# Block 1's mixers: projections in the recurrence's order, six half steps of the inverse among them, unread products taken out

## The chip, the cores and the metric

The kernel runs on one core of one Trainium2 chip. The metric is device microseconds (us) of one execution. Five engines work side by side, each through its own queue and in order: PE (TensorE, matrix products; PEld is its weight load), DVE (VectorE), ACT (ScalarE), POOL (GpSimd) and SP (SyncE, which issues the loads). They wait for each other through semaphores. `ps` is the accumulation memory that products land in, eight banks of 128 x 512 floats; `SB`, `SA`, `HT`, `XT`, `SM` and others are named parts of the on-chip memory.

## What is computed

256 tokens of width 1024 go through two blocks. The first block is a stack of two layers. Each layer projects its input onto the columns of three mixers, runs the mixers, joins their outputs with `w_out`, and ends with a gated feed-forward part:

```python
def first_block(x, ...):
    for l in range(DEPTH):                                   # 2
        h = x @ w_cols
        h_gla, h_rwkv, h_nsa, h_vres = _split(h, ...)
        o_gla = _gla_mixer(gq, gk, gv, gg, galr, ...)        # linear attention, 4 heads, chunks of 64
        o_rwkv = _rwkv7_mixer(rr, rk, rv, ...)               # recurrence, 4 heads, state 64 x 64
        o_nsa = _nsa_mixer(h_nsa, pos, ...)                  # block attention, 8 heads, 2 key heads
        mix = jnp.concatenate([o_gla, o_rwkv, o_nsa], axis=-1) @ w_out[l]
        x = _layer_norm(DEEPNORM_ALPHA * x + mix, ln1_w[l], ln1_b[l])
        ffn = (jax.nn.silu(x @ ffn_w_gate[l]) * (x @ ffn_w_up[l])) @ ffn_w_down[l]
        x = _layer_norm(DEEPNORM_ALPHA * x + ffn, ln2_w[l], ln2_b[l])
    return x
```

The recurrence runs over tokens, `state = state * w_t + sa * b_t + v_t * k_t`. The kernel solves it by chunks of 128 tokens, for which a triangular matrix for each chunk and head is inverted. Block attention is three attentions over the same queries (15 compressed key blocks, selected blocks, a window), each with a gate.

The second block modulates its input by sums over a condition vector (`mod = c @ w_ada + b_ada`), has a mixer of its own, and then a feed-forward part of 32 experts with 4 chosen for each token. All of it is float32.

## The kernel before

**Loads.** SyncE streams all weights through `ring`, four slots of 2 MB, in a fixed order (`ORDER`): for each layer of the first block 7 slots of projections, 2 of the compression, 2 of `w_out`, 11 of gate and up, 6 of down. Twelve slots of the modulation (`ada`) of the second block are put behind slots that `ADA_BEHIND` names; for each, VectorE runs four multiply-and-sum operations (L1704, `modulation_dve`). The condition row that they need is loaded by `condition_sp`, and the rows made of the sums go out through `modulation_rows_sp`, behind a turn on TensorE (`modulation_turn_pe`).

**Projections.** `project_pe` (from L384) makes 15 groups, each a bank of `ps`: weights on the left (L401) for the transposed columns, and for groups 11 to 14 tokens on the left (L418). ScalarE evacuates each (`proj_evac`), and group g needs the evacuation of group g - 4. The columns come in the order linear attention's queries and keys, then the recurrence's R, K, V, ranks, then attention's keys and queries. `rwkv_norm_pe`, `rope_pe` (L1001, the product that rotates keys and queries) and `rwkv_bonus_pe` (L737) stand between the last groups.

**Mixers.** `mixers_pe` (L2571), `mixers_act` and `mixers_dve` write the order of the mixers out by hand. First come eight score products of linear attention (`gla_scores_pe`, L504; VectorE makes a key for each ahead of it, `gla_key_dve`, and masks them all behind the last, `gla_mask_dve`, up to L583), with four pairs of the recurrence's matrices (`rwkv_pairs_pe`, L759) and the compression's hidden layer (`cmp_hidden_pe`, L1048) among them. Then a loop of `STEPS` = 18 steps runs three things side by side:
- the inverse of the recurrence's triangles, for two chunks in turn, in 14 half levels. A half step is a product (`inverse_product_pe`, L858), copied by ScalarE (L892), and an update (`inverse_update_pe`, L877 and L880), added in by VectorE (`inverse_update_dve`, L843). Half levels 0 and 1 are made by masks, 2 to 13 in steps 0 to 11 (`h = s + FIRST_HALF`), and then come six steps of the solve with it: `chunk_removed`, `chunk_solve`, `chunk_out` for each chunk;
- attention in 12 units (`NU`), each four heads of one chunk of queries: 4 with 256 keys, 4 with 128, 4 with the 15 compressed ones. A unit's scores are made in step u + 2 (L1149); VectorE masks them (L1221) or copies them (L1220), ScalarE takes the exponential, VectorE scales them by sum and gate in the next step (L1241 to L1250), TensorE turns them (L1166), ScalarE copies them, and a step later TensorE makes the output (L1177);
- the rest of linear attention in steps 0 to 2.

`clock_pe` (L357 to L360) makes products of constants into a bank whose contents nobody reads; several calls stand in these functions, and they are called fillers below.

Behind the loop the recurrence's output gets its head norm on VectorE (`rwkv_norm_dve`, L457 to L468 and to L972) while TensorE starts `w_out` (L1272): `mix_early_pe` with the six parts k of `EARLY`, which need `gla_out` and `nsa_out`, and `mix_late_pe` with k 2 and 3, which need `rw_out`. Then come layer norm and the gate, up and down products (L1403, L1488), and the next layer, which is the same.

## Time and profile before

| what | us |
|---|---|
| median of 3 runs | 2024.41 |
| the three runs | 2035.28, 2024.41, 2023.99 |
| the profiled execution | 2022.85 |
| its span in the trace | 2021.0 |
| its mean granted TensorE clock | 0.993 |

The profile shows one execution. The span is cut into 40 slices of 50.5 us, and each digit is the busy share of an engine in tenths (DMA is the mean share of the 16 DMA engines, PEclk the clock that TensorE was granted, in tenths of its full 2.4 GHz):

```profile
PE   8999999999999999999999999999999999999997
DVE  2387588774587586764731111111111111111112
PEclk9999999999999999999999999999999999999999
DMA  8440057656630065437299999999999999999996
```

Slices 1 to 10 are layer 0 of the first block, slices 10 to 19 layer 1, then comes the second block's mixer, and from slice 22 on the experts. The chain that ended last, followed back from the last instruction, gives each line's share of the span:

```profile
PE 80%; DMA 15%; DVE 3%; issue 1%; ACT 0%; SPq 0%; DVEq 0%
```

In the rows below, `L858 PE` is line 858 of the kernel on TensorE, `ps<-SB` the program's names for what is written and read, `128*128 128x128` the weights' and the moving operand's shape, and `x8` the number of instructions drawn together. Each float32 product of the program leaves two records.

### The profile page before, as it was taken

What the parts mean: (1) busy time and instruction counts of PE and PEld (TensorE: products, weight loads), DVE (VectorE), ACT (ScalarE), POOL (GpSimd) and SP (SyncE); (2) the same over time, 40 slices, a digit from 0 to 9 for tenths busy, and PEclk for the clock granted to TensorE, in tenths of its full rate; (3) what the DMA queues carried; (4) which work ended last, traced back from release to release, by engine and by line L of the source; (5) the groups of instructions that cost most, each with busy time, mean ns of one, the idle gap of its engine ahead of it and who ended that gap; (6) DMA issues with size and microseconds to landing.
All of it is one profiled execution on the core that took longest, in us unless ns stands there. A gap on an engine that the chain in (4) does not pass through costs nothing.

```text
span 2021.0 us, 24513 instructions
## 1 busy us (share of the span) xinstructions
PE 1965.7 (97%) x9835; PEld 1113.9 (55%) x9835; DVE 854.5 (42%) x1538; ACT 313.5 (16%) x725; POOL 45.1 (2%) x62
## 2 busy tenths in 40 slices
PE   8999999999999999999999999999999999999997
PEld 7867588848878588748653333333333333333332
DVE  2387588774587586764731111111111111111112
ACT  1335211101435121102410000000000000000001
POOL 0021000000021000000000000000000000000000
PEclk9999999999999999999999999999999999999999
DMA  8440057656630065437299999999999999999996
GB/s 362 182 163 3 32 219 302 229 208 248 266 153 1 22 240 198 167 134 280 105 363 400 429 427 429 428 428 428 428 429 428 429 428 429 428 428 429 428 428 291
DMA packets 44275, 598.75 MB, mean 296 GB/s; under 512 B 5056, under 2 KB 5360, under 8 KB 8464
## 3 DMA queue, kind: packets, MB, share of 16 engines
q1 hardware_dynamic: 44208, 597.82, 71.9%
q8 instruction: 46, 0.75, 0.1%
q14 instruction: 21, 0.17, 0.0%
HBM read 596.73 MB, written 1.07 MB: 296 GB/s over the span
## 4 chain that ended last, share of the span: by engine, by line
PE 80%; DMA 15%; DVE 3%; issue 1%; ACT 0%; SPq 0%; DVEq 0%
PE ps L2348 18%; DMA ring<-in_stream 15%; PE ps L1403 13%; PE ps L2396 8%; PE ps L401 6%; PE ps L1488 5%; PE ps L2322 3%; PE ps L1272 3%; PE ps L360 2%; PE ps L2337 2%; PE ps L418 2%; PE ps L2433 2%; PE ps L1819 1%; PE ps L1985 1%; PE ps L1149 1%; PE ps L1166 1%
## 5 line engine op out<-in xcount | busy, mean ns | idle before, releaser
L2348 PE MATMUL ps<-ring,HT 128*64 128x512 f32 x2176 | 478.9, 594 | 16.9 <-DMA ring<-in_stream 16.4
L2348 PEld LDWEIGHTS ps<-ring,HT 128*64 128x64 f32 x2176 | 152.9, 137 | 336.4 <-issue 290.9
L2396 PE MATMUL ps<-SB,HT 128*64 128x512 f32 x1088 | 252.4, 618 | 0.9 <-ACT HT L2459 0.9
L2504 DVE TENSOR_SCALAR HT<-ps 128x512 f32<-128x512 f32 x34 | 23.5, 691 | 446.1 <-PE ps L2348 446.1
L2396 PEld LDWEIGHTS ps<-SB,HT 128*64 128x64 f32 x1088 | 77.7, 142 | 172.9 <-issue 172.9
L1403 PE MATMUL ps<-ring,SB 128*128 128x256 f32 x704 | 156.0, 379 | 0.3 <-DVE SB L330 0.3
L2453 ACT ACTIVATE HT<-HT 128x512 f32<-128x512 f32 x34 | 21.4, 630 | 843.6 <-DVE HT L2504 843.6
L1403 PEld LDWEIGHTS ps<-ring,SB 128*128 128x128 f32 x704 | 133.6, 190 | 18.8 <-issue 0.7
L2516 DVE TENSOR_TENSOR HT<-ps,TOK 128x512 f32<-128x512 f32 x34 | 23.5, 691 | 284.6 <-PE ps L2396 284.6
L401 PE MATMUL ps<-SB,ring 128*128 128x256 f32 x576 | 126.5, 382 | 3.4 <-DMA ring<-in_stream 3.4
L401 PEld LDWEIGHTS ps<-SB,ring 128*128 128x128 f32 x576 | 110.3, 192 | 19.3 <-DMA ring<-in_stream 2.5
L1403 PE MATMUL ps<-SB 128*128 128x256 f32 x352 | 80.0, 379 | 0.4 <-ACT SB L345 0.4
L1704 DVE SCALAR_TENSOR_TENSOR ring<-ring,SB 128x1024 f32<-128x1024 f32 x48 | 55.8, 1219 | 43.9 <-DMA ring<-in_stream 43.9
L1403 PEld LDWEIGHTS ps<-SB 128*128 128x128 f32 x352 | 66.7, 190 | 9.8 <-issue 0.8
L2337 PE MATMUL ps<-SA,HT 32*64 32x512 f32 x272 | 69.7, 608 | 0.0
L2433 PE MATMUL ps<-HT 64*128 64x512 f32 x272 | 67.6, 615 | 0.9 <-DVE HT L2516 0.9
L2322 PEld LDWEIGHTS ps<-HT,SA 128*128 128x128 f32 x512 | 59.6, 192 | 13.0 <-DVE HT L2442 13.0
L2322 PE MATMUL ps<-HT,SA 128*128 128x128 f32 x512 | 64.0, 278 | 0.0
L1488 PE MATMUL ps<-ring,HT 128*128 128x512 f32 x132 | 60.4, 592 | 0.0
L1272 PE MATMUL ps<-ring,SB 128*128 128x512 f32 x128 | 56.4, 596 | 1.6 <-DVE SB L2709 1.6
L360 PE MATMUL ps<-CST 128*128 128x256 f32 (+2 forms) x190 | 52.0, 393 | 0.0
L2442 DVE TENSOR_TENSOR HT<-ps,COND 128x512 f32<-128x512 f32 x32 | 22.1, 691 | 68.5 <-PE ps L2322 68.5
(489 smaller groups left out, 2249.0 us busy)
## 6 DMA issues: line engine op xcount, KB each, us to landing
ring<-in_stream SPq DMA_DIRECT2D x210, 2048.0 KB, 17.5
SB<-in_stream SPq DMA_DIRECT2D x68, 2048.0 KB, 25.6
SB<-in_ln SPq DMA_DIRECT2D x8, 512.0 KB, 6.9
CST<-in_const SPq DMA_DIRECT2D x1, 1362.0 KB, 5.3
PAR<-in_layer SPq DMA_DIRECT2D x2, 558.5 KB, 11.6
X<-in_x SPq DMA_DIRECT2D x1, 1024.0 KB, 4.9
SB<-in_cond_row SPq DMA_DIRECT2D x2, 512.0 KB, 5.3
HN<-in_head_norm SPq DMA_DIRECT2D x2, 512.0 KB, 12.5
```

The costliest lines, as they stand in the source:

```text
L360: pe.matmul(ps[:, b, at:at + width], ident, cst("pairs")[:, 0:width], start=True, stop=True)
L401: m = pe.matmul(ps[:, proj_bank(g), j * T:(j + 1) * T], w[:, k, (2 * (g % 2) + j) * P:(2 * (g % 2) + j + 1) * P], XT[:, k, :], start=k == ...
L418: m = pe.matmul(ps[:, proj_bank(g0 + t), 0:n], XT[:, k, t * P:(t + 1) * P], w[:, k, a:a + n], start=k == 0, stop=k == KT - 1)
L1272: m = pe.matmul(ps[:, 2 * t + c, :], OT[:, k, t * P:(t + 1) * P], w[:, k, :], start=start and k == ks[0], stop=stop and k == ks[-1], skip_ ...
L1403: ins = pe.matmul(gate_products(f, (m,)), left[:, k, :], right[:, k, :], start=k == 0, stop=k == 3)
L1488: ins = pe.matmul(ps[:, DOWN_BANK[m], :], left, right, start=s + q == 0, stop=s == 5)
L1704: ins = nc.vector.scalar_tensor_tensor(out=w[:, b, :], in0=w[:, b, :], scalar=1.0, in1=CB, op0=ALU.mult, op1=ALU.mult, accum_out=ACC[:, 4 ...
L2322: m = pe.matmul(ps[:, 2, (k % 4) * P:(k % 4 + 1) * P], HF[:, t, k * P:(k + 1) * P], EP0[:, t, :, :].rearrange("p a s -> p (a s)"), start=t ...
L2337: pe.matmul(ps[HD * half:HD * (half + 1), a, :], EOW[0:NE, q, :], BGU[0:NE, half, a, :], start=True, stop=False, skip_group_check=True)
L2348: m = pe.matmul(ps[HD * half:HD * (half + 1), a, :], XE[:, 2 * b + k, q * SLOTS_E:(q + 1) * SLOTS_E], w[:, k, a, half, :], start=False, st ...
L2396: m = pe.matmul(ps[HD * c:HD * (c + 1), 3, :], EHT[:, k, HD * b:HD * (b + 1)], w[:, k, c, :], start=b + k == 0, stop=b + k == 4, skip_grou ...
L2433: m = pe.matmul(ps[:, 4 + 2 * t + c, :], EPT[rows, t * P:(t + 1) * P], EY[rows, :], start=False, stop=True, skip_group_check=True)
```

## The change

- **Columns and groups.** The weights' columns are put in the order R, K, V, ranks, one compression value, then linear attention's queries and keys, then attention's. VectorE's first step on the recurrence (`mix_dve`) waits for five evacuations instead of seven.
- **Projections interleaved.** New functions `projections_pe`, `projections_act` and `projections_dve` write the order of the projections out by hand. Between groups 7 to 14 stand the recurrence's norm, bonus and pairs, the four rotations (all through bank 4 now), the first half levels, and half steps 2 and 3.
- **Mixers.** Half steps 4 to 7 stand between the eight score products. The loop starts at half step 8 (`LOOP_HALF`) and has 16 steps; the solve's six steps stand in steps 6 to 11. The recurrence's norm is in VectorE's step 12 (`BACK - 2`), its way back in TensorE's step 14, and the first `w_out` part in step 15.
- **`w_out`.** The early parts are k 0 to 3 now, for three of four quarters, and wait for `rw_out` and `gla_out`; the late ones are k 4 to 7 and the whole last quarter, and wait for `nsa_out`. Other banks of `ps` take them.
- **Fillers.** All calls of `clock_pe` go, but for one in `chunk_removed_pe`.
- **Modulation.** One block instead of two stands in layer 0's projections, behind the third slot; the others move to layer 0's gate stage, layer 1's projections and layer 1's gate stage, and none stands in layer 0's down projection. The turn of the sums and SyncE's rows move from layer 1's gate stage to its down projection.
- GpSimd's masks of the half levels lose their waits for attention; the compression's blocks move to another place in memory.

The core of the diff:

```diff
-ADA_BEHIND = {("in", 0, 1): (0, 1), ("gu", 0, 2): (2,), ("gu", 0, 4): (3,), ("gu", 0, 6): (4,), ("gu", 0, 8): (5,),
-              ("dn", 0, 0): (6,), ("dn", 0, 1): (7,), ("in", 1, 1): (8, 9), ("in", 1, 3): (10, 11)}
+ADA_BEHIND = {("in", 0, 2): (0,), ("gu", 0, 2): (1,), ("gu", 0, 4): (2,), ("gu", 0, 5): (3,), ("gu", 0, 7): (4,), ("gu", 0, 8): (5,),
+              ("in", 1, 1): (6, 7), ("gu", 1, 2): (8,), ("gu", 1, 4): (9,), ("gu", 1, 6): (10,), ("gu", 1, 8): (11,)}
...
+                if name == "in" and l == 0 and s == 2:
+                    condition_sp(sp)
                 if name == "gu" and s == 1:
                     norm_params(sp, 2 * l)
-                    if l == 0:
-                        for done in ("gla_out", "rw_out", "nsa_out"):
-                            sp.wait_ge(S(done), 1)
-                        condition_sp(sp)
-                if name == "gu" and s == 4 and l == DEPTH - 1:
+                    for done in ("gla_out", "rw_out", "nsa_out"):
+                        sp.wait_ge(S(done), l + 1)
+                    condition_sp(sp)
+                if name == "dn" and s == 4 and l == DEPTH - 1:
                     modulation_rows_sp(sp)
...
-            v.wait_ge(S("proj_evac"), 15 * l + 7)
+            v.wait_ge(S("proj_evac"), 15 * l + 5)
...
-                pe.wait_ge(S("proj_evac"), 15 * l + 13)
+                pe.wait_ge(S("proj_evac"), 15 * (l + 1))
...
-            if s == 2:
-                pe.wait_ge(S("cmp_x"), l + 1)
...
-        EARLY = (0, 1, 4, 5, 6, 7)
-
-        def mix_early_pe(pe, l, t, c, ks=EARLY):
+        def mix_early_pe(pe, l, t, c):
+            pe.wait_ge(S("rw_out"), l + 1)
+            pe.wait_ge(S("gla_out"), l + 1)
+            mix_part_pe(pe, l, t, c, range(4), True, False)
+
+        def mix_late_pe(pe, l):
             pe.wait_ge(S("nsa_out"), l + 1)
-            mix_part_pe(pe, l, t, c, ks, ks[0] == 0, False)
-
-        def mix_late_pe(pe, l):
-            pe.wait_ge(S("rw_out"), l + 1)
-            for t in range(NT):
-                for c in range(2):
-                    if (t, c) == (1, 0):
-                        mix_early_pe(pe, l, 1, 1, EARLY[3:])
-                    m = mix_part_pe(pe, l, t, c, (2, 3), False, True)
-                m.then_inc(S("mix_ready"), 1)
+            mix_part_pe(pe, l, 0, 0, range(4, 8), False, True)
+            mix_part_pe(pe, l, 0, 1, range(4, 8), False, True).then_inc(S("mix_ready"), 1)
+            mix_part_pe(pe, l, 1, 1, range(4, 8), False, True)
+            mix_part_pe(pe, l, 1, 0, range(8), True, True).then_inc(S("mix_ready"), 1)
...
-        FIRST_HALF, HALF_LEVELS, ATT_LAG = 2, 14, 2
-        STEPS = HALF_LEVELS - FIRST_HALF + 6
+        FIRST_HALF, LOOP_HALF, HALF_LEVELS, ATT_LAG = 2, 8, 14, 2
+        STEPS = NU + 2 + ATT_LAG
         CMP_TURN, CMP_OUT, GLA_NORM, GLA_BACK = 0, 1, 1, 2
+        BACK = NU + ATT_LAG
...
+        def inverse_step_pe(pe, l, h):
+            inverse_product_pe(pe, l, h + 1)
+            inverse_update_pe(pe, l, h)
+
+        def projections_pe(pe, l):
+
+            for g in range(0 if l == 0 else 2, 7):
+                project_group_pe(pe, l, g)
+            gla_gate_pe(pe, l)
+            rwkv_ranks_pe(pe, l)
+            project_group_pe(pe, l, 7)
+            rwkv_norm_pe(pe, l)
+            project_group_pe(pe, l, 8)
+            rope_pe(pe, l, 0)
+            project_group_pe(pe, l, 9)
+            rwkv_bonus_pe(pe, l)
+            rwkv_pairs_pe(pe, l, 0)
+            project_group_pe(pe, l, 10)
+            rwkv_pairs_pe(pe, l, 2)
+            rope_pe(pe, l, 1)
+            project_group_pe(pe, l, 11)
+            rwkv_pairs_pe(pe, l, 4)
+            project_group_pe(pe, l, 12)
+            rope_pe(pe, l, 2)
+            rwkv_pairs_pe(pe, l, 6)
+            inverse_first_pe(pe, l, 0)
+            project_group_pe(pe, l, 13, range(4))
+            inverse_first_pe(pe, l, 1)
+            project_group_pe(pe, l, 13, range(4, KT))
+            rope_pe(pe, l, 3)
+            inverse_product_pe(pe, l, FIRST_HALF)
+            project_group_pe(pe, l, 14, range(2))
+            inverse_step_pe(pe, l, 2)
+            project_group_pe(pe, l, 14, range(2, 5))
+            inverse_step_pe(pe, l, 3)
+            project_group_pe(pe, l, 14, range(5, KT))
+            rwkv_current_pe(pe, l)
+
         def mixers_pe(pe, l):
-            pe.wait_ge(S("rope"), ROPE_PIECES * l + 2)
-            for u in range(8):
-                gla_scores_pe(pe, l, u)
-                if u % 2 == 0:
-                    rwkv_pairs_pe(pe, l, u)
-                if u == 0:
-                    rwkv_current_pe(pe, l)
-                if u + 2 < ROPE_PIECES:
-                    rope_pe(pe, l, u + 2)
-                    clock_pe(pe, 0, 384, P, 4)
-                else:
-                    pe.wait_ge(S("rope"), ROPE_PIECES * l + 3)
-                    clock_pe(pe, 7, 0, 256, 1)
+            gla_scores_pe(pe, l, 0)
+            inverse_step_pe(pe, l, 4)
+            gla_scores_pe(pe, l, 1)
+            gla_scores_pe(pe, l, 2)
+            inverse_step_pe(pe, l, 5)
+            gla_scores_pe(pe, l, 3)
+            gla_scores_pe(pe, l, 4)
             cmp_hidden_pe(pe, l, 0)
-            inverse_first_pe(pe, l)
+            inverse_step_pe(pe, l, 6)
+            gla_scores_pe(pe, l, 5)
+            gla_scores_pe(pe, l, 6)
             cmp_hidden_pe(pe, l, 4)
-            inverse_product_pe(pe, l, FIRST_HALF)
+            inverse_step_pe(pe, l, 7)
+            gla_scores_pe(pe, l, 7)
             for s in range(STEPS):
                 u, at = s - ATT_LAG, NU * l + s - ATT_LAG
-                h = s + FIRST_HALF
+                h = s + LOOP_HALF
...
+                elif j < 2:
...
+                if s == BACK + 1:
+                    mix_early_pe(pe, l, 0, 0)
...
+                if s == BACK:
+                    back_pe(pe, 2 * l + 1, R_XC, 5)
+            mix_early_pe(pe, l, 0, 1)
+            mix_early_pe(pe, l, 1, 1)
...
+        def projections_dve(v, l, I, L):
+            mix_dve(v, l, I, L)
+            rwkv_square_dve(v, l, I, L)
+            gla_bias_dve(v, l, I)
+            rwkv_prepare_dve(v, l, I, L)
+            rwkv_mask_dve(v, l, 0)
+            rwkv_mask_dve(v, l, 1)
+            rope_dve(v, l, 0, I, L)
+            rwkv_mask_dve(v, l, 2)
+            rwkv_mask_dve(v, l, 3)
+            inverse_first_dve(v, l, 0)
+            rope_dve(v, l, 1, I, L)
+            rwkv_mask_dve(v, l, 4)
+            rwkv_mask_dve(v, l, 5)
+            gla_decay_dve(v, l, I, L)
+            rwkv_mask_dve(v, l, 6)
+            rwkv_mask_dve(v, l, 7)
+            inverse_first_dve(v, l, 1)
+            inverse_turned_dve(v, l, 0)
+            inverse_turned_dve(v, l, 1)
+            rope_dve(v, l, 2, I, L)
+            gla_query_dve(v, l, I)
+            inverse_update_dve(v, l, 2)
+            rope_dve(v, l, 3, I, L)
+            inverse_update_dve(v, l, 3)
             gla_key_dve(v, l, 0)
             gla_key_dve(v, l, 1)
-            rope_dve(v, l, 0, I, L)
-            rope_dve(v, l, 1, I, L)
-            for u in range(8):
-                rwkv_mask_dve(v, l, u)
-                if u == 0:
-                    rwkv_init_dve(v, l, I, L)
-                if u + 2 < NQC:
-                    gla_key_dve(v, l, u + 2)
-                if u + 2 < ROPE_PIECES:
-                    rope_dve(v, l, u + 2, I, L)
-            v.wait_ge(S("rw_mm"), 8 * (l + 1))
-            inverse_first_dve(v, l)
-            inverse_turned_dve(v, l)
+            rwkv_init_dve(v, l, I, L)
+
+        def mixers_dve(v, l, I, L):
+            for h in range(4, 7):
+                inverse_update_dve(v, l, h)
+                gla_key_dve(v, l, 2 * h - 6)
+                gla_key_dve(v, l, 2 * h - 5)
+            inverse_update_dve(v, l, 7)
...
+                if s == BACK - 2:
+                    rwkv_norm_dve(v, l, I, L)
...
-            rwkv_norm_dve(v, l, I, L)
             v.wait_ge(S("back_ps"), 2 * l + 2)
             nc.vector.tensor_copy(OT[:, 2:4, :].rearrange("p c t -> p (c t)"), ps[:, 5, :]).then_inc(S("rw_out"), 1)
+            attention_merge_dve(v, NU * (l + 1), I)
```

What this does to the order of the instructions is shown at three places. Line numbers of the kernel after differ; `x4` counts the program's instructions here, two records each in the trace.

**TensorE, the last projections (L418, group 13) and the first scores of linear attention (L504).** L1001 is a rotation, L737 turns the recurrence's operands, L745 sums its bonus, L759 a pair of the recurrence, L360 a filler. Before:

```order
L418 MATMUL ps<-ring,SB 128x512 x8
L737 MATMUL ps<-CST,SB 128x128 x4
L504 MATMUL ps<-HT,SA 128x32 x4
L759 MATMUL ps<-SB 128x256 x4
L745 MATMUL ps<-PAR,SB 128x4 x4
L1001 MATMUL ps<-HT,CST 128x256 x2
L360 MATMUL ps<-CST 128x128 x4
```

After, at the same group (L399 is the projection, L790 a first half level's turn, L970 a rotation, L833 a half step's product, L850 and L853 its update):

```order
L399 MATMUL ps<-ring,SB 128x512 x4
L790 MATMUL ps<-CST,SB 128x128 x4
L399 MATMUL ps<-ring,SB 128x512 x4
L970 MATMUL ps<-HT,CST 128x256
L833 MATMUL ps<-SB 128x128 x4
L399 MATMUL ps<-ring,SB 128x512 x2
L833 MATMUL ps<-SB 128x128 x4
L850 MATMUL ps<-SB 128x128 x4
L853 MATMUL ps<-SB 128x128 x4
L399 MATMUL ps<-ring,SB 128x512 x3
```

The filler and the scores are gone from here, and half steps stand between the quarters of the last two groups.

**TensorE, a step of the loop amid the attention units with 128 keys.** L1149 is the scores, L360 a filler, L858 a half step's product, L877 and L880 its update, L1177 the output and L1166 the turn of earlier units. Before:

```order
L1149 MATMUL ps<-HT 128x128 x4
L360 MATMUL ps<-CST 128x256
L858 MATMUL ps<-SB 128x128 x4
L877 MATMUL ps<-SB 128x128 x4
L880 MATMUL ps<-SB 128x128 x4
L1177 MATMUL ps<-SA,NV 64x256 x4
L1166 MATMUL ps<-CST,SA 128x128 x4
```

After (L1118 scores, L888 the solve's product in place of a half step, L1146 output, L1135 turn):

```order
L1118 MATMUL ps<-HT 128x128 x4
L888 MATMUL ps<-SB 128x64 x4
L1146 MATMUL ps<-SA,NV 64x256 x4
L1135 MATMUL ps<-CST,SA 128x128 x4
L1118 MATMUL ps<-HT 128x128 x4
```

The step keeps the scores, output and turn, and has four products of the solve instead of a filler and a half step of twelve.

**VectorE, the recurrence's head norm (L457 to L468 and on) and the last attention units.** L1250 is the scaling of a unit, L1256 the merge of attention's outputs, L952 a copy of the solve. Before:

```order
L1250 TENSOR_TENSOR SA<-SA,SM 128x4x15
L958 TENSOR_SCALAR SB<-ps,SM 64x64 x4
L946 COPY SB<-ps 128x256
L1256 COPY SB<-ps 128x4x128 x2
L952 COPY SB<-ps 128x256
L457 TENSOR_REDUCE SM<-ps 128x8
L458 TENSOR_SCALAR SM<-SM 128x8
L459 TENSOR_TENSOR SB<-ps,SM 128x512
```

After (L945 is the end of the norm, which starts 12 rows ahead at L438; L1184 masks a unit's scores, L1192 to L1219 scale it):

```order
L945 TENSOR_TENSOR SB<-SB 128x512
L1184 TENSOR_TENSOR SA<-ps,CST 128x4x15
L1192 TENSOR_REDUCE SM<-SA 128x4
L1201 TENSOR_SCALAR SM<-SM 128x4
L1210 RECIPROCAL SM<-SM 128x4
L1214 TENSOR_TENSOR SM<-SM,SB 128x4
L1217 TENSOR_SCALAR SM<-SM,CST 128x4
L1219 TENSOR_TENSOR SA<-SA,SM 128x4x15
```

Before, the norm stands behind the last scaling and the merge. Now it stands ahead of the last two units' scaling.

## Rows read from the trace of the kernel before

**Rows 1.** The page's busy times of the engines, share of span, instructions.
```profile
PE 1965.7 (97%) x9835; PEld 1113.9 (55%) x9835; DVE 854.5 (42%) x1538; ACT 313.5 (16%) x725; POOL 45.1 (2%) x62
```

**Rows 2.** Table by stage: window, us; engines' busy us (count); PEclk, DMA share, GB/s.
```profile
569.40:594.30 24.90, 24.26 (x251) 18.03 (x250) 18.23 (x33) 6.18 (x15) 11.12 (x20) 1.00 0.29 96
594.30:674.80 80.50, 78.78 (x650) 64.82 (x650) 59.62 (x132) 41.21 (x131) 9.72 (x8) 1.00 0.12 50
1100.00:1990.00 890.00, 865.37 (x4142) 319.26 (x4140) 154.80 (x335) 49.90 (x93) 0.00 (x0) 0.99 1.01 428
```

**Rows 3.** Time line of TensorE, layer 1: start, us, line, [idle before <-releaser].
```profile
569.44 0.63 PE L504 MATMUL ps<-HT,SA 64*128 64x32 f32 x8
...
594.35 1.16 PE L858 MATMUL ps<-SB 128*128 128x128 f32 x8 [0.69 <-ACT SB L892]
...
674.83 5.42 PE L1272 MATMUL ps<-ring,SB 128*128 128x512 f32 x12
...
707.75 7.14 PE L1403 MATMUL ps<-ring,SB 128*128 128x256 f32 x32 [0.16 <-DVE SB L330]
```

**Rows 4.** The same time line: a half step between its ends.
```profile
640.16 1.05 PE L858 MATMUL ps<-SB 128*128 128x128 f32 x8
...
642.93 1.08 PE L1177 MATMUL ps<-SA,NV 128*64 128x256 f32 x8
```

**Rows 5.** Time lines of VectorE and TensorE: mask, units with 256 keys, update.
```profile
592.71 0.68 DVE L583 TENSOR_TENSOR SA<-ps,CST 128x512 f32<-128x512 f32 x1
...
621.52 0.69 DVE L1220 COPY SA<-ps 128x512 f32<-128x512 f32 x1 [1.08 <-PE ps L1149]
...
624.58 1.22 DVE L1250 TENSOR_TENSOR SA<-SA,SM 128x1024 f32<-128x1024 f32 x1
...
625.73 1.28 DVE L843 TENSOR_TENSOR SB<-SB,ps 128x512 f32<-128x512 f32 x2
...
628.07 0.69 DVE L1220 COPY SA<-ps 128x512 f32<-128x512 f32 x1 [1.06 <-PE ps L1149]
...
625.86 1.09 PE L1166 MATMUL ps<-CST,SA 128*128 128x128 f32 x8 [0.50 <-DVE SA L1250]
```

**Rows 6.** The same time lines: units with 128 keys.
```profile
633.42 0.72 PE L1149 MATMUL ps<-HT 64*128 64x128 f32 x8
...
654.68 0.62 PE L1149 MATMUL ps<-SB,HT 64*128 64x15 f32 x8
...
645.30 0.69 DVE L1221 TENSOR_TENSOR SA<-ps,CST 128x512 f32<-128x512 f32 x1 [0.97 <-PE ps L1149]
...
647.23 0.69 DVE L1250 TENSOR_TENSOR SA<-SA,SM 128x512 f32<-128x512 f32 x1
```

**Rows 7.** The same time lines: unit 10's scores, the recurrence's norm.
```profile
660.66 0.62 PE L1149 MATMUL ps<-SB,HT 64*128 64x15 f32 x8
...
682.89 0.69 DVE L457 TENSOR_REDUCE SM<-ps 128x8 f32<-128x512 f32 x1 [7.53 <-PE ps L938]
...
690.31 0.69 DVE L972 TENSOR_TENSOR SB<-SB 128x512 f32<-128x512 f32 x1
```

**Rows 8.** Table by stretch of line 360 alone: PE and PEld busy us.
```profile
569.40:594.30 24.90, 6.30 (x28) 3.88 (x28) 1.00 0.29 96
594.30:674.80 80.50, 13.33 (x48) 8.07 (x48) 1.00 0.12 50
```

**Rows 9.** Time line of TensorE: the start, and two items of the experts.
```profile
10.90 29.36 PE L401 MATMUL ps<-SB,ring 128*128 128x256 f32 x128 [1.27 <-DMA ring<-in_stream]
...
42.36 41.71 PE L401 MATMUL ps<-SB,ring 128*128 128x256 f32 x192 [2.10 <-DMA ring<-in_stream]
...
1167.68 8.74 PE L2396 MATMUL ps<-SB,HT 128*64 128x512 f32 x32
...
1224.70 7.09 PE L2396 MATMUL ps<-SB,HT 128*64 128x512 f32 x32
```

**Rows 10.** TensorE's waits, 400 to 470 us: us in total, times, longest.
```profile
PE ps L1488 <- DVE HT L1465: 2.2, 3, 1.5
```

More of the change, by code:

```diff
@@ new lines, in project_group_pe @@
+        def project_group_pe(pe, l, g, ks=range(KT)):
+            s = min(g // 2, 6) if g < 11 else 5 + (g > 12)
+            need_slot(pe, AT["in", l, s])
+            w = slot(AT["in", l, s]).rearrange("p (k n) -> p k n", k=KT)
+            if g >= 4:
+                pe.wait_ge(S("proj_evac"), 15 * l + g - 3)
+            for j in range(2 if g < 10 else 1):
+                for k in ks:
+                    if g < 11:
+                        at = (2 * (g % 2) + j) * P
+                        left, right, to = w[:, k, at:at + P], XT[:, k, :], slice(j * T, (j + 1) * T)
+                    else:
+                        t, cols = (g - 11) % 2, slice(P, P + 280) if g < 13 else slice(0, 512)
+                        left, right, to = XT[:, k, t * P:(t + 1) * P], w[:, k, cols], slice(0, 280 if g < 13 else 512)
+                    m = pe.matmul(ps[:, proj_bank(g), to], left, right, start=k == 0, stop=k == KT - 1)
+            if ks[-1] == KT - 1:
+                m.then_inc(S("proj_ready"), 1)
@@ L647, in rwkv_ranks_pe @@
                               start=False, stop=True)
+            if l:
+                pe.wait_ge(S("gla_zb"), l + 1)
+                for c in range(2):
+                    m = pe.matmul(ps[:, 4, c * T:(c + 1) * T], par("misc")[M_VR:M_VR + 32, c * P:(c + 1) * P],
+                                  HT[M_VR:M_VR + 32, T_MISC, :], start=True, stop=True)
             m.then_inc(S("rw_z"), 1)
@@ new lines, in inverse_first_dve, with turned_triangle, inverse_first_pe @@
+            v.wait_ge(S("rw_mk"), 12 * l + s + 1)
+            nc.vector.tensor_tensor(TT[:, us, :], MK[:, us, :], idb, ALU.add).then_inc(S("rw_tm"), 1)
+        def turned_triangle(s):
+            return ps[:, (7, 6)[s], :]
+        def inverse_first_pe(pe, l, s):
+            pe.wait_ge(S("rw_bk"), l + 1)
+            pe.wait_ge(S("rw_mk"), 12 * l + s + 1)
+            for i in range(4):
+                m = pe.transpose(turned_triangle(s)[:, i * P:(i + 1) * P], MK[:, 4 * s + i, :], ident)
+            m.then_inc(S("rw_z_ps"), 1)
```

265 lines of the change are left out of this document (93 added, 172 removed).

## Prediction

> **What bounds the kernel now.** The page's busy times first [rows 1]: TensorE is "busy" for 97% of the span, so that number can't say where time is lost, since products whose result nobody reads are in it. The table by stage [rows 2] can. From 1100 to 1990 us the DMA share is 1.01 at 428 GB/s: the experts' weights set the pace, and the change doesn't touch that stage. Its loads start when the blocks ahead have finished, so what a layer gains or loses ahead of it is carried to the end one for one. In the two stretches of the mixers the DMA share is 0.29 and 0.12: something else sets their pace.
>
> The time line of layer 1 shows the stage's marks [rows 3]. (Layer 0 has the same pattern 452.4 us earlier, so each term counts twice.) Up to 569.4 TensorE runs projections back to back without a wait. From 569.44 to 594.35 it runs eight score products of linear attention, four pairs of the recurrence and fillers; at 594.35 the loop of half steps and attention begins; at 674.83 w_out; at 707.75 the feed-forward part.
>
> In that loop TensorE looks full and isn't what paces it. For a unit with 256 keys VectorE starts at 621.52 and starts the next at 628.07 [rows 5]: 6.55 us. The circle is: VectorE copies, masks, reduces and scales until 625.80 (L1250, 624.58 + 1.22); TensorE turns the unit before (625.86, with a wait of 0.50 for just this), makes the next scores, and VectorE goes on. The update of the inverse (L843, 1.28 us) and the half step's products (2.77 us, [rows 4]) lie inside this circle for nothing.
>
> **The change, part by part, for layer 1.**
>
> 1. Six half steps of the inverse go from the loop to places between projections and scores. One costs TensorE 642.93 - 640.16 = 2.77 us [rows 4]. Where they stood, they were covered by the circle above; among the projections TensorE has no hole, so there they cost all of it: 6 x 2.77 = **+16.6**. The projections themselves, the pairs, the rotations and the compression keep their number and size, and their order costs nothing: I followed who waits for whom. The recurrence's first groups are ready after five evacuations, VectorE's preparation runs under groups 7 to 9, and GpSimd's masks under 13 and 14.
>
> 2. The 28 filler records between 569.4 and 594.3 go: 6.30 us of records [rows 8], less the modelled overlap of eight groups, **-5.7**.
>
> 3. New waits. Behind half steps 4, 5 and 6 VectorE runs the update (1.28, [rows 5]) and only then the next key (at most one operation of L1220's size, 0.69, and half of it for the early keys), while TensorE has 0.55 or 1.0 us of scores to cover it. Three waits of about 1.2, 1.5 and 1.0: **+3.7**. Nothing else on TensorE can pass them, since it runs in order.
>
> 4. The mask of the scores (three operations, the last L583 ending 593.39 [rows 5]) was over 1.0 us before the loop's first product at 594.35. Now the last score stands directly ahead of the loop and VectorE has update 7 to do first, so the mask ends 1.9 us behind it; VectorE then goes into the compression's gelu, which is what the loop's second step waits for. I take **+2.8**. A filler that stood ahead of a transpose in the third step goes: -0.4.
>
> Attention starts 16.6 - 5.7 + 3.7 + 2.8 - 0.4 = 17.0 us later.
>
> 5. The four units with 256 keys: the circle has no half step in it, so it stays 6.55: **0**.
>
> 6. The four units with 128 keys take 654.68 - 633.42 = 21.3 us [rows 6] with half steps and fillers; there TensorE is full. Without them the circle decides: VectorE from 645.30 to 647.92 (L1250, 647.23 + 0.69, [rows 6]) = 2.6, turn 0.6, scores 0.65, handovers 0.15: 4.0 us. The first has still a wide unit to scale (5.0), and the one with the solve's output products (2.5 us) 4.3. So 5.0 + 4.0 + 4.4 + 4.0 = 17.4: **-3.9**.
>
> 7. The recurrence's output comes in step 11, amid the four narrow units: 2.2 us of products in a step of 2.9, **+0.9**. Its norm (L457 to L972, 682.89 to 691.00, 8.1 us [rows 7]) ran under w_out's first products. Now VectorE has it in step 12, and the last two attention units are queued behind it; TensorE has nothing but their transposes to do. From the end of unit 10's scores (660.66 + 0.62) to w_out was 13.5 us [rows 3, 7]. It becomes 1.5 (unit 9's scaling) + 8.1 + about 5 us for two units one after the other, the way back and a copy = 14.6: **+1.1**. So the two steps that the loop loses are given back here.
>
> 8. From the first w_out product to the feed-forward part was 32.9 us [rows 3]. The 64 records are 27.5 of it; the solve's last outputs, a filler, a wait for the norm's copy and the way back are now ahead of it: 29.3, **-3.6**.
>
> Sum per layer: 17.0 - 3.9 + 0.9 + 1.1 - 3.6 = **+11.5**.
>
> 9. The clock. Without fillers TensorE stands idle for about 8 us under the norm, and for 1.5 to 3 us in many steps. What the trace has nearest: at the start, behind 5.9 us of nothing, 128 records take 29.4 us where 192 later ones take 41.7 [rows 9], that is 1.6 us lost; and in the expert stage the same 32 records take 8.74 us in one item and 7.09 in another [rows 9], where the granted clock went to 0.5, the 1.2 GHz level, behind short waits: 1.65 us. The bounds are 0 (the granted clock is 1.00 through the layers now) and all TensorE work between 650 and 700 at half rate, 12 us, less what the waits swallow, say 10. I take one loss of 1.6 behind the norm, 1.3 for the two transposes and products right behind it that are on the path, and one dip of 1.65 in the steps: **+4.5**, nearer the low end, as one dip is what the rows show at a time.
> The Trainium skill, "TensorE: Matmul & The Clock Gate", Part 1, says that the half rate is the default and that activity releases it, and it advises against holes between bursts of matmuls. This speaks against taking the fillers out. With it the sum has the 4.5; without it 0 there, and the total would be 9 us lower.
>
> 10. Start of layer 0: the second block of the modulation goes, and the first comes behind the third slot. The wait of 2.10 us at 42.36 [rows 9] goes: **-2.1**, once. In the down projection of layer 0 TensorE waits 2.2 us for sums that VectorE makes late because of modulation blocks [rows 10]; those go: **-2.2**, once. In the gate stage of layer 0 five blocks stand instead of four, two pairs of them in neighbouring steps. VectorE then needs 13.1 us in each where TensorE needs 12.5, and is 4 us ahead: nothing. In layer 1 the four blocks stand as layer 0's did. SyncE's wait for the modulation rows moves to the down projection, ahead of one load that isn't due by then: nothing.
>
> Total: 2 x (11.5 + 4.5) - 2.1 - 2.2 = **+27.7**. Against the profiled execution (time 2022.85, span 2021.0, both in the table of times; 1.6 below the median of the runs) this is 2050.5; I say **2050 us**.
>
> **Rivals.**
> - *The same, and the clock holds.* For it: 1.00 throughout the layers now, and steps that stay more than half full. 2 x 11.5 - 4.3 = +18.7: 2041.
> - *The clock stays low through much of attention.* For it: every step there has a hole now. About 10 a layer in place of 4.5: 2061 to 2066.
> - *TensorE's queue paces the loop after all*, and the waits of 0.5 us are the accident. Then the fillers (13.3 us of records in the loop, [rows 8], and 6.3 ahead of it) come off the path, the half steps cost nothing net, and a layer loses 12 to 18 us: 2022.85 - 30 - 4.3 = about 1985. Against it: the 0.50 wait recurs at the same place in each wide step, and VectorE's circle adds up to the step. It decides from the point where attention starts less than 8 us later.
> - *The norm doesn't hold attention up* (part 7 is off by 8 us) and the waits of part 3 are half: 2 x (11.5 - 8 - 1.9) - 4.3 = -1: about 2022 to 2028.
>
> **Chances.** Forecast 0.50; clock holds 0.26; clock low 0.10; norm free 0.08; TensorE paces 0.06. About 1% (20 us) is what a measurement of this kernel tells from no change; measured from the median 2024.4 the bound lies at 2044.7, inside the spread of the forecast's own case (2041 to 2058), of which I give a tenth to "within". Slower: 0.45 + 0.10 + 0.04 of the clock-holds case = 0.59. Faster: 0.06, and 0.01 of the norm case: 0.07. Same: 0.34. The range takes in the clock-holds case and most of the clock-low one, with 5 us a layer of error in parts 3, 4 and 7 below: 2031 to 2064.
>
> **What would show it.** Part 1: the linear-attention scores begin some 14 us later after the start of the projections than 569.44 - 480. Part 3: TensorE waits of 1 to 1.5 us ahead of the scores, ended by VectorE's key. Part 5: units with 256 keys 6.5 us apart. Part 6: units with 128 keys 4 us apart. Part 7: a TensorE wait of about 8 us ended by L1219, the scaling. Part 9: a granted clock under 1.00 there. Wrong would be: the first attention scores of layer 1 less than 10 us later than now after the projections' start, or an expert stage that takes the shift up.

## The result, and the profile after

The changed kernel takes 2064.53 us (median of 4 executions, 2062.54 to 2068.92). The kernel before took 2024.2 in the same comparison. The ratio is 1.0195, 95% interval 1.0167 to 1.0222: it is slower by 40 us, about 2%. The prediction said 2050 with a range up to 2064. The side was right, the median lies half a microsecond above the range's upper end, and the change cost one and a half times what was forecast.

The page of the profiled execution (2068.92 us, span 2067.1, mean granted clock 0.975 where it was 0.993) shows the busy times that answer to [rows 1], and the row of the granted clock over the 40 slices of the span:

```profile
PE 1962.3 (95%) x9687; PEld 1106.0 (54%) x9687; DVE 852.0 (41%) x1539; ACT 315.2 (15%) x725; POOL 46.1 (2%) x62
PEclk9998899999999799999999999999999999999999
```

Before, all 40 digits were 9. Now slices 4 and 5 (layer 0's mixers) and slice 14 (layer 1's) are lower. In the experts' stage all digits are 9 as before.

The table by stage of TensorE in layer 1 of the kernel after, which answers to [rows 2]. Columns: window, its length, TensorE's busy time (records), granted clock, DMA share, GB/s. The windows run from the start of the projections to the first score, the loop, the first, fifth, ninth and eleventh attention unit's scores, `w_out`, and the feed-forward part:

```profile
486.70:604.90 118.20, 118.20 (x625) 1.00 0.44 175
604.90:634.00 29.10, 25.19 (x258) 0.88 0.34 117
634.00:647.60 13.60, 10.93 (x100) 0.98 0.50 214
647.60:677.50 29.90, 19.96 (x143) 0.84 0.00 1
677.50:697.40 19.90, 19.00 (x141) 0.82 0.01 2
697.40:704.50 7.10, 6.94 (x63) 1.00 0.02 4
704.50:721.50 17.00, 7.01 (x45) 0.62 0.19 61
721.50:753.10 31.60, 31.44 (x77) 0.93 0.06 18
```

In the kernel before every one of these stretches had 1.00. Five of the eight are now well below it. TensorE's waits over the whole execution (engine, what, line <- who, line: us in total, times, longest) name who it stands for:

```profile
PE ps L1135 <- DVE SA L1219: 31.8, 15, 7.5
PE ps L485 <- DVE SA L560: 7.0, 6, 1.4
```

L1135 is the turn of an attention unit, L1219 VectorE's scaling of it (in [rows 5] L1166 and L1250), L485 a score product of linear attention and L560 its key. In the kernel before, the same view has no wait for a key, and for the scaling only six short ones:

```profile
PE ps L1166 <- DVE SA L1250: 2.8, 6, 0.5
```

### The profile page after: what moved, and what is told of

The parts are those of the page before. It is cut to its first block, busy times and chain, and to the rows that moved or that the text cites. A ratio compares the mean times of both kernels' runs of the same rounds, so it can differ in the third digit from the quotient of the medians.

```text
span 2067.1 us, 24237 instructions
## 1 busy us (share of the span) xinstructions
PE 1962.3 (95%) x9687; PEld 1106.0 (54%) x9687; DVE 852.0 (41%) x1539; ACT 315.2 (15%) x725; POOL 46.1 (2%) x62
## 4 chain that ended last, share of the span: by engine, by line
PE 79%; DMA 14%; DVE 5%; issue 1%; ACT 0%; SPq 0%; DVEq 0%
PE ps L2315 17%; DMA ring<-in_stream 14%; PE ps L1372 12%; PE ps L399 9%; PE ps L2363 8%; PE ps L1456 6%; PE ps L2289 3%; PE ps L1244 3%; PE ps L2304 2%; PE ps L2400 2%; PE ps L1786 1%; PE ps L1952 1%; PE ps L1135 1%; PE ps L1118 1%; PE ps L833 1%
## 5 line engine op out<-in xcount | busy, mean ns | idle before, releaser
L2471 DVE TENSOR_SCALAR HT<-ps 128x512 f32<-128x512 f32 x34 | 23.5, 692 | 449.9 <-PE ps L2315 449.9
L2483 DVE TENSOR_TENSOR HT<-ps,TOK 128x512 f32<-128x512 f32 x34 | 23.5, 692 | 281.2 <-PE ps L2363 281.2
L399 PE MATMUL ps<-SB,ring 128*128 128x256 f32 x608 | 135.6, 384 | 1.3 <-DMA ring<-in_stream 1.3
L399 PEld LDWEIGHTS ps<-SB,ring 128*128 128x128 f32 x608 | 116.4, 193 | 18.9 <-issue 3.0
L1135 PE MATMUL ps<-CST,SA 128*128 128x128 f32 (+1 forms) x152 | 28.7, 337 | 34.4 <-DVE SA L1219 31.8
L1157 ACT ACTIVATE SA<-SA,SM 128x256 f32<-128x256 f32 (+2 forms) x112 | 44.8, 402 | 51.4 <-DVE SM L1201 51.4
## 6 DMA issues: line engine op xcount, KB each, us to landing
ring<-in_stream SPq DMA_DIRECT2D x210, 2048.0 KB, 17.4
```

The lines of the kernel that those rows point to most:

```text
L399: m = pe.matmul(ps[:, proj_bank(g), to], left, right, start=k == 0, stop=k == KT - 1)
L1135: m = pe.transpose(ps[0:kw, turn_bank(n, k), j * P:(j + 1) * P], N_P[:, n % 2, j, k * P:k * P + kw], ident)
L1157: nc.scalar.activation(N_P[:, n % 2, j, 0:w], N_P[:, n % 2, j, 0:w], ACT.Exp, scale=HD ** -0.5, bias=MX[:, n % 2, j:j + 1], accum_out=RS[: ...
```

## Where the time went: stage by stage

The table sets the marks of TensorE's time line in layer 1 side by side, each stretch in us. A unit with 256 keys is called wide below, one with 128 keys narrow. The last column is the experiment a_fill below: the changed kernel with unread products in its waits, which hold the granted clock at 1.00 in seven of the eight stretches (it is 0.89 from unit 10 to `w_out`).

| layer 1, from | before | after | a_fill |
|---|---|---|---|
| projections to first score | 104.60 | 118.26 | 118.25 |
| first score to the loop | 24.91 | 29.06 | 25.87 |
| loop to unit 0 | 12.45 | 13.60 | 13.41 |
| 4 units, 256 keys | 26.62 | 29.89 | 26.08 |
| 4 units, 128 keys | 21.26 | 19.95 | 17.44 |
| units 8 and 9 | 5.98 | 7.03 | 7.04 |
| unit 10 to `w_out` | 14.17 | 17.04 | 15.57 |
| `w_out` to feed-forward | 32.92 | 31.59 | 29.55 |
| sum | 242.91 | 266.42 | 253.21 |

In these executions layer 1 costs 23.5 us more than before, not 16.0. The last column divides that: 10.3 us are the new order, where the prediction had 11.5, and 13.2 us are the clock, where it had 4.5. Layer 0 agrees: from its first score to its feed-forward part it takes 138.4 us before, 148.6 after and 135.0 in a_fill, so there the clock is 13.6 us. The profiled execution is the slowest of its four, though; what the medians give stands in the account further below.

What the lower rate does is seen on equal instructions. In the time line of the kernel after (start, us, what, [idle before <-releaser]) a turn and the scores behind it, behind a wait of 2.59 us and then behind one of 2.49:

```profile
660.97 1.94 PE L1135 MATMUL ps<-CST,SA 128*128 128x128 f32 x8 [2.59 <-issue]
662.84 1.79 PE L1118 MATMUL ps<-HT 64*128 64x256 f32 x8
...
669.03 1.09 PE L1135 MATMUL ps<-CST,SA 128*128 128x128 f32 x8 [2.49 <-DVE SA L1219]
670.05 1.13 PE L1118 MATMUL ps<-HT 64*128 64x256 f32 x8
```

The same eight records of the turn took 1.94 us and then 1.09, those of the scores 1.79 and then 1.13. Both lie on the circle that sets the wide units' pace (VectorE's scaling, turn, scores, VectorE again), so that unit was 1.5 us longer. The two waits are nearly equal and only one was followed by the lower rate, so the length of a single wait doesn't tell whether the clock falls behind it.

## The experiments

The theory to be tested was that the shortfall of the forecast is the clock: without the unread products TensorE waits in many steps, the granted clock falls behind these waits, and the records after them are on the path. The rivals: the waits cost what they cost whatever TensorE does in them; or a term of the order (half steps, norm, modulation) was mis-sized.

### Unread products in the waits of the changed kernel

```diff
             gla_scores_pe(pe, l, 1)
+            clock_pe(pe, 0, 384, P, 4)
             gla_scores_pe(pe, l, 2)
...
+                if s in (GLA_BACK, GLA_BACK + 1):
+                    clock_pe(pe, 3, 0, 256, (4, 2)[s - GLA_BACK])
...
                     if u == 1:
+                        clock_pe(pe, 3, 0, 256, 5)
                         pe.wait_ge(S("cmp_kv"), l + 1)
+                    if u in (2, 3):
+                        clock_pe(pe, 6, 0, 256, 5)
+                    if s == BACK - 1:
+                        clock_pe(pe, 5, 256, 256, 14)
                     attention_turn_pe(pe, at - 1)
```

(and 5 and 4 more of the small ones ahead of scores 4 and 6)

> The changed kernel with unread products put back only where TensorE stood waiting in its trace: 4, 5 and 4 small ones between the score products of linear attention, 4 and 2 in steps 2 and 3, 5 in each of the three steps of wide attention units, 14 under the recurrence's norm. They are sized under the waits (1.15, 1.42, 0.95, 2.2, 1.0, 2.6, 2.5, 2.8 and 7.5 us). Theory (the shortfall of the prediction is the clock: in layer 1 the records between 604 and 727 us at the lower rate took some 14 us more than at the full one): the granted clock stays at 1.00 through the layers and the time falls by 2 x 12 to 14, from 2064.5 to 2036 to 2041. Rival (those records are slow for another reason, or the waits hold the path whatever TensorE does in them): 2062 to 2070. A wait for VectorE's key or scaling must shrink by what the products take and the next unit's start must not move in either case.

Measured: 2041.67 us (2037.86 to 2043.60, 10 executions), ratio to before 1.0072 (1.0050 to 1.0094). These are 96 products more (192 records) and 22.9 us less than the kernel after, just short of the 24 to 28 us expected. The clock was 0.993 in the profiled execution. The time line of TensorE in layer 1 has the marks of the last column above:

```profile
469.38 5.52 PE L378 MATMUL ps<-SB,ring 128*128 128x128 f32 x48
...
587.63 0.63 PE L485 MATMUL ps<-HT,SA 64*128 64x32 f32 x8
...
626.91 1.13 PE L1118 MATMUL ps<-HT 64*128 64x256 f32 x8
...
652.99 0.71 PE L1118 MATMUL ps<-HT 64*128 64x128 f32 x8
...
670.43 0.62 PE L1118 MATMUL ps<-SB,HT 64*128 64x15 f32 x8
...
681.53 8.00 PE L360 MATMUL ps<-CST 128*128 128x256 f32 x28
689.36 0.60 PE L1135 MATMUL ps<-CST,SA 128*15 128x128 f32 x4
...
693.04 3.70 PE L1244 MATMUL ps<-ring,SB 128*128 128x512 f32 x8 [0.78 <-DVE SB L2760]
...
722.59 7.41 PE L1372 MATMUL ps<-ring,SB 128*128 128x256 f32 x32 [0.16 <-DVE SB L330]
```

The first eight records of `w_out` took 3.70 us here and 5.75 in the kernel after; the 14 products under the norm delay the turn behind them by 0.3 us (11.89 us after unit 10's scores, 11.61 in the kernel after) and still pay. Their 28 records took 8.00 us, while 10 records of the same size took 2.43 in a wide step of this run, so some of them ran at the lower rate: here the unread products took the dip, and the records behind them did not. The clock theory holds: the same program order with more work in it is faster, and equal records are short again. The time is that of the prediction's rival "the clock holds", 2041.

### Only under the norm

The same kernel with the 14 products of step `BACK - 1` alone.

> The changed kernel with 14 unread products only in the 7.5 us wait under the recurrence's norm. Clock theory: the two turns, outputs and the first eight records of w_out behind it run at the full rate, which is 1.8 + 2.3 us a layer: 2064.5 - 8 = 2056, granted clock 1.00 from unit 11's turn on. Rival (the clock is already down from the wide steps and stays so): no change. Attention's wide steps should stay as slow as they are in either case.

Measured: 2058.66 us (2056.17 to 2061.29, 4 executions), ratio 1.0153 (1.0105 to 1.0200), 5.9 us less than the kernel after, where 8 were expected. The turn behind the norm takes 0.60 us and `w_out`'s first eight records 3.70, at the full rate as expected; the wide steps' waits and their half rate are unchanged. So this place gives back a quarter of the 22.9 us, and the rest lies in the other places, which were not filled one by one.

### The kernel before without its unread products

```diff
-                    clock_pe(pe, 0, 384, P, 4)
...
-                    clock_pe(pe, 7, 0, 256, 1)
```

These two lines are b_nofill_scores; b_nofill takes out the calls in the loop, `inverse_product_pe` and the solve's steps too.

> The kernel before with all its unread products of the mixers taken out and nothing else changed. Theory A (they hold the clock): 5.7 us a layer leave the score stage and about 5 the narrow steps, where TensorE was full, and the clock takes back 5 to 14 a layer: 2015 to 2040. Theory B (the clock isn't worth much, they only cost): 2024 - 2 x 11 = 2002 or lower. The granted clock of the wide steps tells: under 1.00 by A though those steps themselves lose no filler but one.

> The kernel before without the 14 unread products between the score products of linear attention alone. The prediction's part 2 says that they are on TensorE's path: 2 x 5.7 = 11.4 us less, 2013. Rival (VectorE's masks and rotations pace this stage, the products only fill waits): no change, 2024, with waits for VectorE in their place.

Measured: b_nofill 2034.90 (2025.39 to 2042.59, 10 executions), ratio 1.0041 (1.0016 to 1.0066); b_nofill_scores 2032.51 (2030.21 to 2043.43, 10 executions), ratio 1.0032 (1.0007 to 1.0056). Taking 28 records a layer off TensorE's queue, with nothing else changed, made the kernel slower by 8 us in the median, where both expectations of that run had it no slower. Its time line in layer 1's score stage:

```profile
579.44 1.13 PE L759 MATMUL ps<-SB 64*128 64x256 f32 x8 [1.18 <-DVE SB L777]
580.40 0.53 PE L504 MATMUL ps<-HT,SA 64*128 64x32 f32 x8
582.33 1.92 PE L504 MATMUL ps<-HT,SA 64*128 64x32 f32 x16 [1.39 <-DVE SA L575]
584.02 2.09 PE L759 MATMUL ps<-SB 64*128 64x256 f32 x8
...
592.95 3.64 PE L1048 MATMUL ps<-ring,SB 128*32 128x256 f32 x32
...
598.19 1.93 PE L1048 MATMUL ps<-ring,SB 128*32 128x256 f32 x32
```

Behind two waits of 1.18 and 1.39 us the same pair of the recurrence (L759) takes 2.09 us in place of 1.13, and 32 records of L1048 take 3.64 us where the next 32 take 1.93. So part 2 of the prediction, which booked these records as a gain of 5.7 us, holds only while the clock does. In b_nofill the table of windows (busy time and instructions of TensorE, its weight loads, VectorE, ScalarE and GpSimd, then the granted clock, DMA share and GB/s) has the score stage at 0.57, and the loop's third step with the first wide units at 0.88:

```profile
580.00:600.00 20.00, 18.75 (x156) 15.17 (x160) 12.04 (x22) 2.72 (x6) 3.76 (x6) 0.57 0.03 10
612.00:640.00 28.00, 21.51 (x145) 17.11 (x143) 21.06 (x38) 11.68 (x33) 5.09 (x4) 0.88 0.02 9
```

### Which of them are pure cost

b_trim keeps the products of the first two scores, of steps 2 and 3 and the last ahead of `w_out`, and drops twelve products a layer behind which b_nofill showed short waits or none.

> The kernel before with only those unread products taken out behind which TensorE showed no wait when they all went: the six between the later score products of linear attention (0.63 us each), and six of the narrow attention steps (0.53 each). Kept are the 8 small ones at the first two scores, those in steps 2 and 3, and the last ones ahead of w_out. If they are pure cost: 2 x (3.8 + 2 to 3.2) less, 2010 to 2013, at a granted clock of 1.00 in the layers. Rival (the score stage's small products don't hold the clock by themselves): granted clock near 0.6 for part of it again, and 2024 to 2032.

Measured: 2025.71 us, ratio 0.9997 (0.9970 to 1.0023), which is no difference; but the ten executions go from 2013.07 to 2040.03, and the mean clock with them: 2013.07 at 0.996; 2021.34, 2021.71 and 2022.94 at 0.987; five more at 2025.5 to 2030.5 with 0.985 to 0.989; 2040.03 at 0.978. The profiled one is the first. In it the clock held at 1.00 through layer 1's mixers, and most of the sum came: the narrow units take 19.76 us in place of 21.26, and the score stage 22.39 in place of 24.91, which is 2.5 us less and not 3.8, since two waits for VectorE's keys (1.10 and 0.55 us) came up. The other executions have a lower mean clock; where it fell in them no trace shows. The products that looked like pure cost kept most executions of the kernel at nearly the same clock.

### Half steps back under the circle

a_fill_half6 tests parts 1 and 5: it takes half steps 6 and 7 from between the scores into the loop (`LOOP_HALF = 6`), and the norm to step `BACK`. The unread products stand as in a_fill, but for those of the two wide steps that now have a half step, and the 14 go with the norm. Against the kernel after, the lines that move the half steps and the norm:

```diff
-            inverse_step_pe(pe, l, 6)
...
-            inverse_step_pe(pe, l, 7)
...
-        FIRST_HALF, LOOP_HALF, HALF_LEVELS, ATT_LAG = 2, 8, 14, 2
+        FIRST_HALF, LOOP_HALF, HALF_LEVELS, ATT_LAG = 2, 6, 14, 2
...
-                if s == BACK - 2:
+                if s == BACK:
                     rwkv_norm_dve(v, l, I, L)
```

> The kernel a_fill with half steps 6 and 7 taken from between the score products back into the loop (LOOP_HALF = 6, so the solve's steps come two later and the recurrence's norm moves to VectorE's step 14), and with the unread products of the wide steps left out where half steps now stand. By parts 1 and 5 of the prediction two half steps among the scores cost 2 x 2.77 us a layer, and under VectorE's circle nothing: 2041.7 - 11 = 2031, less 2 to 4 more for the waits for keys that go, plus 1 to 2 a layer if the later norm ends later. Wide units must stay 6.5 us apart. Rival (a half step in the loop costs there what it saves here, TensorE's queue paces the wide steps): wide units 2 to 3 us further apart in two steps, and 2039 to 2043.

Measured: 2041.82 us, ratio 1.0061 (1.0036 to 1.0087), no gain in the median, and two groups of executions: five at 2033.6 to 2038.6 (clock 0.991 to 0.994) and five at 2045.0 to 2047.6 (0.985 to 0.987). The profiled one is of the second. Its time line in layer 1 shows the order doing what was forecast, wide units 6.5 us apart with whole half steps in them, then four waits, and its table of windows the clock after them:

```profile
583.95 0.64 PE L485 MATMUL ps<-HT,SA 64*128 64x32 f32 x8
...
603.61 1.16 PE L833 MATMUL ps<-SB 128*128 128x128 f32 x8
...
617.59 1.13 PE L1118 MATMUL ps<-HT 64*128 64x256 f32 x8
...
630.57 1.13 PE L1118 MATMUL ps<-HT 64*128 64x256 f32 x8
...
637.12 1.13 PE L1118 MATMUL ps<-HT 64*128 64x256 f32 x8
...
643.66 0.72 PE L1118 MATMUL ps<-HT 64*128 64x128 f32 x8
...
647.64 1.09 PE L1135 MATMUL ps<-CST,SA 128*128 128x128 f32 x8 [1.35 <-DVE SA L1219]
```

```profile
640.00:660.70 20.70, 15.67 (x142) 1.00 0.01 2
660.70:689.50 28.80, 28.12 (x147) 0.51 0.12 37
```

From the first score to the loop it was 19.7 us (603.61 - 583.95) against 25.9 in a_fill: two half steps of 2.77 and a wait less. From unit 0 to unit 4 it was 26.07 against 26.08: two half steps more, at no cost. That confirms parts 1 and 5. a_fill_half6n puts seven products into the four waits:

```diff
+                    if s in (6, 7):
+                        clock_pe(pe, 6, 0, 256, 2)
+                    if s in (8, 9):
+                        clock_pe(pe, 5, 256, 256, s - 7)
                     attention_turn_pe(pe, at - 1)
```

> The kernel a_fill_half6 with 2, 2, 1 and 2 unread products more, in steps 6 to 9, where the narrow attention units left TensorE waiting 1.35, 1.10, 0.68 and 1.11 us in its trace and the clock fell behind them. Clock theory (its executions at 2034 are those in which the clock held, those at 2045 those in which it fell in the narrow steps): all executions at 2033 to 2037, clock 0.99 or more, and against a_fill (2041.7) 6 us less, which is two half steps a layer off the path less a little. Rival (the spread has another source, two half steps are worth nothing): 2041 or both groups again.

Measured: 2035.54 us (2032.98 to 2038.11, 10 executions), ratio 1.0040 (1.0019 to 1.0062). The second group is gone, and the median is 6.1 us under a_fill's, where the sum of the two half steps is 11 (2 x 2 x 2.77). The rival that half steps are worth nothing has fallen. The marks of layer 1 show where the rest went. Against a_fill the score stage is 6.2 us shorter (19.65) and the narrow units 0.4. But the stretch from the loop to unit 0 is 0.6 longer, units 8 and 9 are 0.9 longer, and the stretch from unit 10 to `w_out`, where the later norm stands, is 2.1 longer (17.67 in place of 15.57).

### The modulation alone

b_ada is the kernel before with the diff's `ADA_BEHIND`, its places of `condition_sp`, `modulation_turn_pe` and `modulation_rows_sp`, and nothing else of the change.

> The kernel before with nothing but the modulation's new places (one block behind the third slot, none in layer 0's down projection, the turn and the rows in layer 1's down projection). Part 10 of the prediction: the 2.10 us wait of TensorE at 42 us and the 2.2 us of waits in layer 0's down projection go, 2024.4 - 4.3 = 2020. Rival (other waits take their place, in the gate stages where blocks stand closer): 2024 or more, and TensorE waits for VectorE's sums in a gate stage.

Measured: 2019.20 us (2017.57 to 2023.24, 12 executions), ratio 0.9965 (0.9947 to 0.9983): 5.2 us faster than before, where part 10 said 4.3. The wait at 42 us is gone from its start, one row of 320 records in place of two [rows 9]; L1488 ([rows 10]) no longer stands among TensorE's waits:

```profile
10.86 71.52 PE L401 MATMUL ps<-SB,ring 128*128 128x256 f32 x320 [1.28 <-DMA ring<-in_stream]
82.31 1.13 PE L492 MATMUL ps<-HT,PAR 16*128 16x256 f32 x4
```

This is the one part of the change that pays by itself, and by its median the fastest version here. An attempt at more, b_ada_tail, dropped six unread products a layer of the narrow steps from it.

> The kernel b_ada with six of the unread products in the narrow attention steps taken out as well (those at the score products stay). If TensorE's queue paces the narrow steps and the clock holds there: units with 128 keys 0.4 to 0.5 us closer, 2 x 2 to 2.5 us in all, 2014 to 2015. Rival (the narrow steps then have waits and the clock falls behind them in part of the executions): 2019 to 2028 with a wide spread, the mean clock at 0.985 in the slow ones.

Measured: 2021.27 us, ratio 0.9972 (0.9949 to 0.9996), 2013.15 to 2030.78 in 12 executions. Its best execution is 4.4 us under b_ada's best, about the 4 to 5 forecast; its median is 2.1 above b_ada's, with the wide spread that the rival named.

## Why the prediction was right, and where it fell short

- **Parts 1 and 5** (six half steps on the path, +16.6; wide units 0): the first score came 13.66 us later after the projections' start, forecast 14. a_fill's wide units took 26.08 in place of 26.62, and the move of two half steps confirmed both. Right.
- **Parts 2 to 4** (+0.4 together, attention 17.0 later with part 1): at full clock 15.6 later, so they came to -1.0. The three waits for keys were 1.15, 1.42 and 0.95 us, forecast 1.2, 1.5 and 1.0. From the loop to unit 0, where the exposed mask was booked, it was +0.96 and not +2.4.
- **Part 6** (units with 128 keys 17.4): 17.44 in a_fill. (The text of part 6 has 4.3 for the step that its sum takes as 4.4; it took 4.41.) **Part 7** (+0.9 and +1.1): +1.06 and +1.40, with the wait under the norm at 7.48 us, forecast about 8. **Part 8** (29.3): 29.55. Right, at full clock.
- **Part 10** (-4.3): -5.2 measured alone. Right.
- **Part 9 is the step that failed**, by its size: "I take one loss of 1.6 behind the norm, 1.3 ..., and one dip of 1.65 in the steps: +4.5, nearer the low end, as one dip is what the rows show at a time". It was 13.2 a layer in the profiled execution and 11.4 by the medians (22.9 / 2), both more than the upper bound of 10. By stretches (after less a_fill): 3.2 from the first score to the loop, 3.8 in the wide units, 2.5 in the narrow ones, 1.5 ahead of `w_out`, 2.0 in it.

  What the bound left out: it had counted TensorE's work only from 650 to 700 us. But part 3 of the same text had forecast waits of 1 to 1.5 us in the score stage, and part 5 had taken the half step of 2.77 us out of each wide step and left nothing in its place; the first dips came there. The trace of before couldn't show it: in its mixers TensorE's longest wait was 0.8 us, since unread products stood in the longer ones, as the waits of 1.18, 1.79 and 2.59 us in b_nofill's trace show. A trace in which the cover is whole can't tell how often the clock falls without it, and the bound should have taken in every stretch in which the text itself forecast a wait.

  One of the two rows that part 9 went by is also no evidence of the clock: at the start of the program, where it counts 1.6 us lost, the granted clock of before's trace is 1.00 in every us, so what made those records long is open.

So what came is the rival "the clock stays low through much of attention", 2061 to 2066, to which I had given 0.10, and not the case that was called likeliest. (The sum of another rival, TensorE paces, is 2022.85 - 30 - 4.3 = 1988.6 and not about 1985; nothing hangs on it.)

The rule of the Trainium skill ("TensorE: Matmul & The Clock Gate", Part 1), that the half rate is the default and activity releases it, was weighed in the prediction at 9 us over the whole program. The traces agree with it in this: with unread products in the waits the half rate is nearly gone, and that is worth 22.9 us. They agree only in part on the release: in b_nofill_scores the half rate went on through 14.2 us in which TensorE was busy all the time (last section).

**The account.** The order and the modulation give 2 x 10.3 - 5.2 = 15.4 us. The profiled executions of a_fill and of the kernel before differ by 15.2 (2038.05 - 2022.85), their medians by 17.3; the 2 us between are the spread, since a_fill's profiled execution lies 3.6 under its median and that of before 1.5. The clock is 22.9 by the medians of a_fill and the kernel after, which makes up the 40.3 measured. Between their profiled executions it is 30.9. Of these, 26.8 lie between the first score and the feed-forward part of the two layers (13.6 and 13.2). Another 2.2 lie in the first 224 records of the projections of layer 0 (50.80 us against 48.59, at a granted clock of 1.00 in both, so not shown to be the clock), and 1.1 in layer 0's feed-forward and down products. The remaining 0.8 stand ahead of these records and behind the last mark. So the terms of the table are those of one slow execution, and a layer's clock loss at the median is nearer 11 than 13 us.

## What to carry to other kernels

Before taking unread products out, find which of them stand in a wait and which in a full queue, and put the clock of every stretch that will have waits into the bound, not of the one where the longest wait is. Work that looks free to remove on TensorE may be what keeps its rate, and a version without it can show its price as a wide spread from execution to execution rather than in its best time, as b_trim and b_ada_tail did. And where VectorE's circle set the pace, TensorE's work inside it was free here: work moved out of it to a full stretch was paid in whole.

## What was not expected of the hardware

Waits of 1.18 and 1.39 us between small products were enough, in b_nofill_scores, for the granted clock to go to its 1.2 GHz level and stay there over 14 us of work without a wait, as its table of windows shows (window, length, TensorE's busy time, granted clock, DMA share, GB/s):

```profile
582.30:596.50 14.20, 14.18 (x112) 0.50 0.01 2
```

Such waits don't always do it. In b_trim's profiled execution waits of 1.10 and 0.55 us stand in the same stage and the granted clock stays at 1.00, and in the kernel after one of two waits of 2.5 us was followed by the full rate. Even in the kernel before, the wait of 0.56 us ahead of the expert's products is the same in both items of [rows 9], of which one then went at 0.5 for some 3 us and the other stayed at 1.00.

In b_trim, 0.018 of mean clock went with 27 us of time. The kernel before has the same thing in small: of its 77 executions beside the experiments, 58 lie at 2022.1 to 2027.7 us with a clock of 0.992 to 0.996, and 19 at 2033.6 to 2038.2 with 0.987 to 0.990.
